# A two-layer transformer trunk on one core: the later blocks of both up projections computed as seven half-size products

## What is computed

```python
h = rms_norm(x, ffn_norm[i])                       # (512, 1024)
a, gate = jnp.split(h @ w_up, 2, axis=-1)          # w_up: (1024, 2 * 2816)
a = causal_conv_of_3_taps(a, conv_w) + conv_b      # along the tokens, each channel alone
x = x + (jax.nn.silu(a) * gate) @ w_down           # w_down: (2816, 1024)
```

## Time and profile before

| | |
|---|---|
| median of 3 runs | 1130.2 us (1130.11 to 1130.2) |
| the profiled execution | 1129.55 us, span of the trace 1127.8 us |
| PE busy | 1116.1 us, 99% of the span |
| DVE busy | 718.6 us, 64% |
| ACT busy | 477.1 us, 42% |
| POOL busy | 3.2 us |
| DMA | 101.98 MB, mean 90 GB/s, 29.2% of the 16 engines' span |

### The profile page before, as it was taken

One profiled execution on the slowest core, in us unless ns is written; L12 is line 12 of the kernel. 1 busy time (PEld: TensorE's weight loads), 2 busy tenths in 40 slices (PEclk: granted clock), 3 DMA queues, 4 the chain that ended last, 5 costly groups with the idle time before them and its releaser, 6 DMA issues.

```text
span 1127.8 us, 15482 instructions
## 1 busy us (share of the span) xinstructions
PE 1116.1 (99%) x5544; PEld 957.1 (85%) x5544; DVE 718.6 (64%) x1240; ACT 477.1 (42%) x954; POOL 3.2 (0%) x20
## 2 busy tenths in 40 slices
PE   8999999999999999999999999999999999999997
PEld 8999888888888888888999999788888888888886
DVE  6888775655656553337787888857565565656435
ACT  6788653222222232235666766544222122232224
POOL 1000000000000000000000000000000000000000
PEclk9999999999999999999999999999999999999999
DMA  6311043232332222325311111043323323122232
GB/s 207 102 63 51 1 150 112 74 112 85 101 109 77 74 75 95 104 99 168 113 56 58 56 59 55 4 129 111 112 75 111 97 89 112 57 75 93 93 102 103
DMA packets 144862, 101.98 MB, mean 90 GB/s; under 512 B 12121, under 2 KB 137270, under 8 KB 144822
## 3 DMA queue, kind: packets, MB, share of 16 engines
q1 hardware_dynamic: 144798, 101.45, 29.2%
q10 hardware_dynamic: 24, 0.01, 0.0%
HBM read 99.34 MB, written 2.10 MB: 90 GB/s over the span
## 4 chain that ended last, share of the span: by engine, by line
PE 93%; DVE 4%; ACT 1%; issue 1%; DMA 0%; SPq 0%; DVEq 0%
PE ps L590 24%; PE ps L591 24%; PE ps L592 23%; PE ps L666 16%; PE ps L707 2%; PE ps L889 2%; PE ps L908 1%; PE ps L768 1%; DVE w_lo L1685 0%; DMA x_tok<-in_x 0%; DVE h_lo L1717 0%; ACT w_hi L1213 0%; DVE xT L2049 0%; DVE x_tok L2276 0%; DVE ssacc L1710 0%
## 5 line engine op out<-in xcount | busy, mean ns | idle before, releaser
L1213 ACT ACTIVATE w_hi<-raw 128x512 fp32r<-128x512 f32 (+2 forms) x204 | 192.1, 969 | 295.4 <-PE ps L592 292.8
L590 PE MATMUL ps<-h_hi,w_lo 128*128 128x512 f32 x704 | 274.3, 390 | 0.0
L591 PE MATMUL ps<-h_lo,w_hi 128*128 128x512 f32 x704 | 274.3, 390 | 0.0
L592 PE MATMUL ps<-h_hi,w_hi 128*128 128x512 f32 x704 | 274.3, 390 | 0.0
L1685 DVE TENSOR_TENSOR w_lo<-raw,w_hi 128x512 fp32r<-128x512 f32 (+2 forms) x204 | 222.8, 1114 | 16.6 <-ACT w_hi L1213 16.4
L590 PEld LDWEIGHTS ps<-h_hi,w_lo 128*128 128x128 f32 x704 | 132.2, 188 | 27.7 <-issue 0.3
L591 PEld LDWEIGHTS ps<-h_lo,w_hi 128*128 128x128 f32 x704 | 132.2, 188 | 27.5
L592 PEld LDWEIGHTS ps<-h_hi,w_hi 128*128 128x128 f32 x704 | 132.2, 188 | 27.3
L2087 DVE TENSOR_TENSOR normed<-ps,rstd 128x512 f32<-128x512 f32 x44 | 30.4, 692 | 160.5 <-PE ps L592 155.0
L666 PE MATMUL ps<-w_hi,h_lo 128*128 128x384 f32 x368 | 126.3, 343 | 0.2
L666 PE MATMUL ps<-w_hi,h_hi 128*128 128x384 f32 x368 | 125.9, 342 | 0.0
(11 more groups left out here) (210 smaller groups left out, 1599.6 us busy)
## 6 DMA issues: line engine op xcount, KB each, us to landing
raw<-in_ffn_w_up SPq DMA_DIRECT2D x88, 512.0 KB, 4.6
raw<-in_ffn_w_down SPq DMA_DIRECT2D x44, 512.0 KB, 3.2
raw<-in_b_w_in SPq DMA_DIRECT2D x24, 512.0 KB, 4.7
raw<-in_a_w_in SPq DMA_DIRECT2D x3, 1024.0 KB, 7.6
raw<-in_a_w_out SPq DMA_DIRECT2D x2, 1536.0 KB, 7.1
raw<-in_b_w_out SPq DMA_DIRECT2D x2, 1536.0 KB, 6.4
raw<-in_a_w_in SPq DMA_DIRECT2D x8, 256.0 KB, 7.1
out<-x_tok SPq DMA_DIRECT2D x8, 256.0 KB, 2.0
```

The source lines that it names most:

```text
L590: pe.matmul(out_, a_lo, b_hi, start=start, stop=False)
L591: pe.matmul(out_, a_hi, b_lo, start=False, stop=False)
L592: return pe.matmul(out_, a_hi, b_hi, start=False, stop=stop)
L1213: act.activation(w_hi[:, s, at], raw[:, s, at], ACT.Copy).then_inc(hi_done, 1)
```

## The change

The last 8 blocks of layer 0's up projection and the last 16 of layer 1's (PLAIN = 14 and 6 blocks stay as they were) are computed by Strassen's scheme in its seven-product form. Here the 2x2 split is: rows, `a` against `gate`; the inner dimension, inputs 0 to 511 against 512 to 1023; columns, tokens 0 to 255 against 256 to 511. Four weight combinations (S1 to S4) and four combinations of the normed input (T1 to T4) are needed beside the plain quarters.

- POOL's queue builds S1 to S4 in DRAM (`w_sums`) by DMAs that copy and DMAs that accumulate: `weight_sums` is called 4 times for layer 0 and 8 times for layer 1, each with eight DMAs of 512 KB in four steps, each step waiting for the one before. They begin once POOL's constants are issued.
- A block in the new form is `seven_products`: seven products of 4 `hi_lo` of 256 columns, so 84 matmuls, into four banks. SP loads for it 24 slices of weights of 64 KB in three DMAs (`load_seven`) and 4 more for S4 (`load_fourth`); the first of each layer waits for that layer's sums.
- ACT makes the high parts (3072 and 512 columns a block), copies one product out of PSUM (`m1_from`), and does the first tap of the convolution and Silu. DVE makes the low parts (two of 1536 columns, one of 512), and adds the products up (`outputs`, five instructions), two taps, and the gated product.
- During the last six plain blocks of each layer, DVE writes the input with the norm applied (`normed_h`, 8 instructions of 512 columns), four differences (`t_source`, 1024 columns), and ACT and DVE the high and low parts of seven operands of 1024 columns (`op_high`, `op_low`). Four of these replace `h_hi` and `h_lo` piece by piece while the last plain block runs, which is for that walked kc by kc.
- The load of the final gain moves from the start of layer 1's up projection to the end of it. The first pair of the down projection in layer 0 takes its banks in another order, and its waits follow `c12_done`.

The diff, cut to its core:

```diff
+PLAIN = (14, 6)
...
+HT = T // 2
+QC = HK * P
+HALF_D = D // 2
+OPERANDS = ("B11", "B21", "B22", "T3", "T2", "T1", "T4")
+NEGATED = ("T1", "T2")
+SUM_COLS = 1024
...
+                conv_first = sb("conv_first", [P, T], F32, st_n)
+                s4_hi = sb("s4_hi", [P, QC], F32R, st_n)
+                gated_first = sb("gated_first", [P, T], F32, st_n)
+                s4_lo = sb("s4_lo", [P, QC], F32R, st_n)
             conv = sb("conv", [P, 2, T], F32, st)
             gated = sb("gated", [P, 2, T], F32, st)
...
             sink_in = sb("sink_in", [P, UA * 4], F32, st)
             angcos = sb("angcos", [P, NT, HALF], F32, st)
+
...
+
+        op_hi = {"B11": pair_of(u_hi, 0), "B21": b21_ops[:, 0, :], "B22": b22_ops[:, 0, :]}
+        op_lo = {"B11": pair_of(u_lo, 0), "B21": b21_ops[:, 1, :], "B22": b22_ops[:, 1, :]}
+        for n, o in enumerate(OPERANDS[3:]):
+            op_hi[o], op_lo[o] = pair_of(h_hi, n), pair_of(h_lo, n)
+        op_hi = {o: quarter(a) for o, a in op_hi.items()}
+
+        hn = u_all[:, FB - KC:FB, :]
+
+        def hn_block(i, j):
+
...
+            def load_seven(l, s, f):
+
+                if is_block(f, PLAIN[l], PLAIN[l] + 1):
+                    sp.wait_ge(lo_done, part_done(f"up{l}", f - 2))
+                    sp.wait_ge(sum_landed, sums_in(l))
+                else:
+                    sp.wait_ge(wlo_done, nth(l, f) * 2 - 4)
+                rv = raw[:, s, :].rearrange("p (k n) -> p k n", n=P)
+                sp.dma_start(rv[:, 0:HK, :], wv[:, HK:KC, bass.ds(f * P + F, P)]).then_inc(raw_landed[s], 16)
+                sp.dma_start(rv[:, HK:HK + KC, :], wv[:, :, bass.ds(f * P, P)]).then_inc(raw_landed[s], 16)
+                sp.dma_start(rv[:, HK + KC:, :], sv[:, 0:3 * HK, bass.ds(f * P - PLAIN[l] * P, P)])\
+                  .then_inc(raw_landed[s], 16)
+                if is_block(f, PLAIN[l]):
+                    load_fourth(l, f)
+                elif not is_block(f, PLAIN[l] + 1):
+                    load_fourth(l, f - 1)
+
...
+                if ph == "down1":
+                    sp.wait_ge(products_done, nth(1, FB - 1))
                     sp.dma_start(gain_end.rearrange("p a b -> p (a b)"), final_norm.partition_broadcast(P))\
                       .then_inc(gain_end_landed, 16)
...
+                elif ph[:2] == "up":
+                    l = layer(ph)
+                    with sp.Fori(1, PLAIN[l] // 2) as r:
+                        for s in range(2):
+                            load(ph, s, r, "own")
+                    for s in range(2):
+                        load_seven(l, s, PLAIN[l] + s)
+                    with sp.Fori(PLAIN[l] // 2 + 1, FB // 2) as r:
+                        for s in range(2):
+                            load_seven(l, s, r * 2 + s)
+                    load_fourth(l, FB - 1)
...
@@ -581,6 +714,35 @@
+
+            def weight_sums(l, rows, c, done):
+
+                wv, sums = ffn_w_up[l], w_sums[l]
+                a, gate = PLAIN[l] * P + c, PLAIN[l] * P + c + F
+
+                def part(half, at):
+                    return wv[half * HALF_D + rows:half * HALF_D + rows + P, at:at + SUM_COLS]
+
+                s1, s3, s2, s4 = (sums[q * HALF_D + rows:q * HALF_D + rows + P, c:c + SUM_COLS] for q in range(4))
+                pool.dma_start(s1, part(1, gate)).then_inc(sum_landed, 16)
+                pool.dma_start(s3, part(0, a)).then_inc(sum_landed, 16)
+                pool.dma_start(s2, part(0, a)).then_inc(sum_landed, 16)
+                pool.dma_start(s4, part(1, a)).then_inc(sum_landed, 16)
+                pool.wait_ge(sum_landed, done + 4 * 16)
+                pool.dma_start(s1, part(0, gate), accum_op=ALU.add, max_dma_last_dim=4 * SUM_COLS).then_inc(sum_landed, 16)
+                pool.dma_start(s3, part(0, gate), accum_op=ALU.add, max_dma_last_dim=4 * SUM_COLS).then_inc(sum_landed, 16)
+                pool.wait_ge(sum_landed, done + 6 * 16)
+                pool.dma_start(s2, s1, accum_op=ALU.add, max_dma_last_dim=4 * SUM_COLS).then_inc(sum_landed, 16)
+                pool.wait_ge(sum_landed, done + 7 * 16)
+                pool.dma_start(s4, s2, accum_op=ALU.add, max_dma_last_dim=4 * SUM_COLS).then_inc(sum_landed, 16)
+                pool.wait_ge(sum_landed, done + 8 * 16)
+
+            done = 0
+            for l in range(2):
+                for c in range(0, (FB - PLAIN[l]) * P, SUM_COLS):
+                    for rows in range(0, HALF_D, P):
+                        weight_sums(l, rows, c, done)
+                        done += 8 * 16
 
 
...
                     order = [(g, kc) for g in range(2) for kc in range(KC)]
                     for g, kc in order:
                         if is_first and s == 0 and g == 0:
...
+                        if is_last and s == 1 and g == 1 and kc in (1, 3, 5):
+                            ins.then_inc(h_left, 1)
                     ins.then_inc(up_done, 1)
+
+            def product(l, f, bank, half, w_high, w_low, o):
+
+                if is_block(f, PLAIN[l]):
+                    pe.wait_ge(oplo_done, len(OPERANDS) * l + OPERANDS.index(o) + 1)
+                out_ = ps[:, bank, half * HT:(half + 1) * HT]
+                for kc in range(HK):
+                    c = slice(kc * P, (kc + 1) * P)
+                    ins = hi_lo(out_, w_high[:, c], w_low[:, c], op_hi[o][:, kc, :], op_lo[o][:, kc, :],
+                                start=(kc == 0), stop=(kc == HK - 1))
+                return ins
+
+            def seven_products(l, s, f):
+
+                pe.wait_ge(wlo_done, nth(l, f) * 2)
+                if is_block(f, PLAIN[l] + 1):
+                    pe.wait_ge(u_done, FB * l + PLAIN[l])
+                elif not is_block(f, PLAIN[l]):
+                    pe.wait_ge(c12_done, nth(l, f) - 2)
+                at = 4 - 4 * s
+
+                def part(n):
+                    return w_hi[:, s, n * QC:(n + 1) * QC], w_lo[:, s, n * QC:(n + 1) * QC]
+
+                product(l, f, at, 0, *part(1), "B11")
+                product(l, f, at, 1, *part(4), "T3").then_inc(first_bank, 1)
+                product(l, f, at + 1, 0, *part(2), "B21")
+                product(l, f, at + 1, 1, *part(5), "T2")
+                product(l, f, at + 2, 1, *part(3), "T1")
+                product(l, f, at + 2, 0, *part(0), "T4")
+                pe.wait_ge(s4lo_done, nth(l, f))
+                product(l, f, at + 3, 0, s4_hi[:, :], s4_lo[:, :], "B22").then_inc(products_done, 1)
 
             def down_pair(l, r, is_first, is_last):
 
...
-                    order = [(0, dc) for dc in [*range(h, KC), 0, 1]] + [(1, dc) for dc in range(h, KC)] + \
-                            [(0, 2), (0, 3)] + [(1, dc) for dc in range(h)]
+                    order = [(s, dc) for s in range(2) for dc in [*range(h, KC), *range(h)]]
...
-                    if is_first and s == 0 and bank in (0, 2):
-                        pe.wait_ge(u_done, FB * (l + 1) - (1 if bank == 0 else 0))
+                    if is_first and s == 0 and bank in (0, KC // 2):
+                        pe.wait_ge(c12_done, nth(l, FB - 1 if bank == 0 else FB - 2))
...
-                with pe.Fori(1, FB // 2) as r:
+                with pe.Fori(1, PLAIN[l] // 2 - 1) as r:
                     up_pair(l, r, False)
+                up_pair(l, PLAIN[l] // 2 - 1, False, True)
+                for s in range(2):
+                    seven_products(l, s, PLAIN[l] + s)
+                with pe.Fori(PLAIN[l] // 2 + 1, FB // 2) as r:
+                    for s in range(2):
+                        seven_products(l, s, r * 2 + s)
...
+            def seven_high(l, s, f):
+
+                else:
+                    act.wait_ge(products_done, nth(l, f) - 2)
+                act.activation(w_hi[:, s, :], raw[:, s, :], ACT.Copy).then_inc(whi_done, 1)
+
+            def fourth_high(l, f):
+
+                act.wait_ge(s4_landed, nth(l, f) * 16)
+                if is_block(f, PLAIN[l]):
+                    act.wait_ge(u_done, FB * l + PLAIN[l])
+                else:
+                    act.wait_ge(products_done, nth(l, f) - 1)
+                act.activation(s4_hi[:, :], s4_raw[:, :], ACT.Copy).then_inc(s4hi_done, 1)
+
+            def m1_from(l, s, f):
+
+                act.wait_ge(first_bank, nth(l, f))
+                if is_block(f, PLAIN[l]):
+                    act.wait_ge(u_done, FB * l + PLAIN[l])
+                else:
+                    act.wait_ge(c12_done, nth(l, f) - 1)
+                act.activation(m1_kept, ps[:, 4 - 4 * s, 0:HT], ACT.Copy).then_inc(m1_out, 1)
+
+            def first_tap(l, f):
+
+                act.wait_ge(c12_done, nth(l, f))
+                act.wait_ge(u_done, f + FB * l)
+                act.activation(conv[:, 0, :], normed[:, 0, :], ACT.Identity,
+                               bias=vecT[:, l, bass.ds(f + R_CONVB, 1)],
+                               scale=vecT[:, l, bass.ds(f + (R_CONVW + 2 * FB), 1)]).then_inc(c0_done, 1)
...
+                            high(up, s, r + 1, (up, r * 2 + s))
```

(113 more changed lines are left out.)

205 lines of the change are left out of this document (165 added, 40 removed).

## The result

The changed kernel takes 1145.2 us (median; 1143.35 to 1146.12), the kernel before beside it 1130.15 (1130.03 to 1130.2). The ratio is 1.013, with an interval of 1.0114 to 1.0149. The forecast of 1117.3 us is 28 us too low and the range ends 14 us short. The profiled execution took 1143.35 us, its span is 1141.6 us.

A forecast was written before the change was run, and what follows sets the result against it. PE, busy 99%, was taken as the bound: 1129.55 - 21.1 (products) + 3.5 (passages) + 4.5 (start) + 0.2 (entries) = 1116.65 us, with the median 0.65 above, so 1117.3; range 1108 to 1131.

The forecast's parts named there:

- What bounds the kernel: Whole kernel: PE is the bound, busy 99% of the span at full clock.
- The products: New blocks: 84 matmuls at 119 ns take 10.00 us instead of 10.88; 24 blocks save 21.1 us, bounds 19.2 to 23.2.
- the rival of 125 ns: New blocks: weight loads pace long streams; slower above 125.5 ns a matmul, 1135.3 us at 128 ns; chance 0.08.
- the one of 113.5: New blocks: 256 columns cost half of 512, 113.5 ns; 32.4 us saved, 1106.0 us in all; chance 0.03.
- DVE: New blocks: DVE works 9.3 us, 9.5 with seeing PE's end, of 10.0, and just stays behind PE.
- The passage: Last plain block into new form: PE waits 1.5 us in layer 0, 2.1 in layer 1; together 3.5, bounds 1 and 6.
- The start: First microseconds: 2 MB of the sums' copies share full DMA engines with x and the weights, costing 4.5 us.
- the bound of 8: Start of the kernel: upper bound of the cost, 8 us, if accumulating DMAs join the copies.
- The sums beside the new blocks: Sums ready without a wait, 16 to 61 us a call; new blocks' loads take 0.63 of the DMA engines, covered.
- The rival "the sums are late": Layer 0: a call over 71 us makes PE stand still, at 90 us a call it waits 70 us; chance 0.05.
- The entries to the down projections: Layer 0: PE steps 0.4 instead of 0.23 us; layer 1 covered by transposes; net +0.2 us.
- the gain's load: End of layer 1's up projection: the moved load waits on SP ahead of the third down block's weights, costing nothing.

The follow-up runs named there:

- e8: e2 with DVE making the second low part of 1536 columns twice in every new block; 1129.53 us, ratio 0.9996.
- e6: e5 with T4's low part moved behind the gate of the last plain block; 1111.71 us, ratio 0.9836.
- e10: The changed kernel with the accumulating DMAs replaced by plain copies of the same size, order and waits; 1134.41 us, ratio 1.0037.
- e2: The changed kernel without its sums, their slices read from ffn_w_up with the same loads; 1114.27 us, ratio 0.986.
- e5: The changed kernel with sums begun at about 32 us and layer 1's last five calls held until its attention's second unit is projected; 1114.46 us, ratio 0.9859.
- e3: The changed kernel with all sums held past the start and layer 1's sums held until layer 0's last new block is done; 1124.66 us, ratio 0.9962.
- e9: The changed kernel with all sums held until the eighth low part of the weights, about 32 us; 1134.24 us, ratio 1.0042.
- e1: The changed kernel with layer 1's eight calls of sums held until layer 0's last new block is done; 1135.3 us, ratio 1.0047.
- e4: The kernel before with the same 96 DMAs of the sums added on POOL, results never read; 1146.19 us, ratio 1.0148.

## Why the prediction was wrong, step by step

**What bounds the kernel: right.** PE was the bound, and where the sums don't disturb it, it still is (layer 1).

**The products: right, at the edge of its bounds.** The steps are 120.0 ns (mean of 1336 from 850 to 1014 us), not 119. Timeline of PE of after, 18 steps apart:

```profile
959.82 0.28 PE L754 MATMUL ps<-h_hi,w_hi 128*128 128x256 f32 x1
...
961.98 0.28 PE L754 MATMUL ps<-h_hi,w_hi 128*128 128x256 f32 x1
```

A block takes 10.08 us and saves 0.80, 24 of them 19.2, which is the lower bound that stood there. Neither the rival of 125 ns nor the one of 113.5 came true. The Trainium skill's 109 ns (TensorE: Matmul & The Clock Gate, section Back-to-back issue gap) is not seen in a long stream either: 120 is 10% above it. That section gives its formula for isolated matmuls and says that in a stream of weight loads and matmuls both set the spacing; the prediction left this out when it held the formula against its 119.

**DVE: right in sign, too dark in size.** Timeline of DVE, one new block of layer 1 in after, from its first instruction to the next one's, 10.08 us later:

```profile
933.50 0.69 DVE L2456 TENSOR_TENSOR normed<-ps,normed 128x512 f32<-128x512 f32 x1 [1.17 <-PE ps L754]
...
936.89 1.76 DVE L2443 TENSOR_TENSOR w_lo<-raw,w_hi 128x1536 fp32r<-128x1536 f32 x1
...
943.58 0.69 DVE L2456 TENSOR_TENSOR normed<-ps,normed 128x512 f32<-128x512 f32 x1 [1.10 <-PE ps L754]
```

DVE waits 1.1 to 1.2 us for PE in a block. The prediction had 0.5, with another 0.2 until it sees PE's end; so its 9.3 us of work are some 0.4 too many, a little from each instruction. Against a plain block, where DVE idles 3.9 us, this cover is thin, and e8 shows its end.

**The passage: right in cause and size.** Gaps of 1.4 to 1.6 us in each layer, against 1.5 and 2.1. In layer 0 of after it is 1.65, with late loads in it. The extra 0.6 of layer 1 did not come. Timeline of DVE there, after (T4's low part, then the gate):

```profile
852.36 1.23 DVE L2434 SCALAR_TENSOR_TENSOR h_lo<-u_all,h_hi 128x1024 fp32r<-128x1024 f32 x1 [0.40 <-ACT h_hi L1724]
853.51 0.68 DVE L2391 TENSOR_TENSOR normed<-ps,rstd 128x512 f32<-128x512 f32 x1
```

e6 swaps these two and the gap goes. The prediction priced this wait and called it a cost of the change; it could have asked which of the two is needed first.

**The start: right in kind, half in size.** 9.5 us instead of 4.5, beyond the bound of 8. The delay of the loads was put somewhat low, at 4 to 5.5 us: PE's wait at 18.63 is 5.8 us, for weights whose high part ACT can only make at 16.74 (9.94 before). By then POOL had issued four plain copies and no accumulating DMA, so the reason that stood beside the bound of 8, accumulating DMAs, is not the one, and e10 agrees. What comes on top is first the clock: PE leaves the wait at 1.2 GHz, in the stretch 20 to 24 us the granted clock is 0.50, and 15 matmuls are done there where it was 26. Steps of 384 columns are 0.32 us instead of 0.17. A gap on PE has a price behind it, and the sum had none. The rest, a bit over 1 us, lies in short waits for later loads.

**The sums beside the new blocks: the step that failed.** The prediction asked whether the sums are *ready* in time, bounded a call between 16 and 61 us, and took no wait. The call took 39 us, inside the bounds, and nobody ever waited for a sum. It then priced a new block's loads at 0.63 of the DMA engines (0.60 measured) and called them covered, "A load has more than 10 us from its release to ACT". That holds for the three large loads of a block. S4's has 6.8 us, since it has one buffer, and just this load is the one that came late. The prediction never put the sums' traffic beside that of the blocks. Twelve calls of 39 us are 470 us, so the other eight run from 135 to 475. Even at the middle of the bounds they reach into layer 0's new blocks, which begin at about 328. There the DMA engines are 0.97 full, S4's loads on the chain take 10 to 15 us, and 18.3 us are lost that the sum did not hold. No run gave S4 a second buffer, so how much of this a longer lead would have saved is not shown. The rival "the sums are late" had the wrong victim: it asked who waits for the sums, and not who waits because of them.

**The entries to the down projections, and the gain's load: nothing to be seen.** The sum held 0.2. In e2 the step of the landmarks over layer 0's down projection is +0.01, and that from the start of layer 1's to the last matmul +0.04. In e6 the products and the passages give -19.2 + 0.4 = -18.8 against -18.4 measured.

With the sums of the changed kernel out of the way (e2, e5), the same working gives 1130.2 - 19.2 + 2.8 = 1113.8, and 1114.3 and 1114.5 were measured. The forecast, with 4.5 us for the start, stood 3 above that. **Open** stays why single runs of e3, e9 and e10 lie 9 to 13 us apart and those of e5 and e6 within about 1. Every version in which sums meet uncovered loads scatters (the changed kernel by 2.8 us, e1 and e4 by 5), but one profile of each can't show what differs. Of the 1.9 us at 186.14 I know that the sums of squares on DVE run 12.1 us behind e5's while PE runs 9.9 behind, and have not followed it further.

## What to carry to other kernels

Price a background transfer by every stretch it runs through, not only by its deadline: add its share of the DMA engines to that of the work beside it (here to some 1.13), and look for the one load there that has the shortest lead. The same 50 MB cost 31 us in one place and nothing in another. When a new form of the work needs less of the bound engine, first look at what it takes from the others (here DVE's idle time falls from 3.9 to 1.2 us a block, and the load of S4 has 6.8 us where a plain block's loads are asked for a block ahead), for that is what the next disturbance meets. Where two instructions stand in a row on an engine that is off the path, put the one that is needed first in front: that was worth 2.75 us for one moved line.
